# A hybrid decoder step on one core: prompt attention with a logits buffer per query tile, and its masks and divisions issued in rows

## The chip, the cores and the metric

The kernel runs on one core of a Trainium2 chip. The core has a matmul engine (TensorE, PE in the profile), a vector engine (VectorE, DVE), a scalar engine (ScalarE, ACT), GpSimd (POOL) and a sync engine (SyncE, SP) that here only starts transfers. The metric is the device time of one execution in microseconds, as the median over runs.

## The reference, cut to what matters

Two layers, each with four head groups side by side, an output projection and a mixture of experts. The change concerns group A, sparse attention, for a prompt of 512 tokens and for a sample group of 8 sequences with 4 new tokens and 512 cached keys each.

```python
def dsa_attend(q, qi, wi, k, v, ki, q_pos, topk):
    dots = jnp.einsum('bthd,bsd->bths', qi.astype(f32), ki.astype(f32)) * IDX_DIM ** -0.5
    score = jnp.einsum('bth,bths->bts', wi.astype(f32), jax.nn.relu(dots))
    ...
    _, sel = lax.top_k(score, topk)
    ...
    logits = jnp.einsum('bthd,btkhd->bthk', q.astype(f32), k_sel.astype(f32)) * A_HEAD_DIM ** -0.5
    logits = jnp.where(valid[:, :, None, :], logits, -jnp.inf)
    p = jax.nn.softmax(logits, axis=-1)
    return jnp.einsum('bthk,btkhd->bthd', p.astype(v.dtype), v_sel)
```

Group B (a recurrence called rwkv below) ends with a norm over its heads, `y = ((y - mu) * rsqrt(var + eps)) * g + b`, a bonus and a gate. Its last steps are interleaved with the attention in the code.

## The kernel before

Each engine runs a program of its own, written out by hand; order on an engine is program order, and engines meet at named semaphores. There is no scheduler. `m.*` are fixed places in one SBUF arena, `ps` is the PSUM with 8 banks.

The selected keys are a bias (0 or a large negative number) that is added to dense logits. The prompt has 4 query tiles of 128 tokens; tile i looks at i + 1 key tiles, for 4 heads. Its steps are:

- `logits(i)` on PE (L1051): 4 matmuls into `ps` banks 0 to 3.
- `masked(i)` on DVE (L2239 for tiles 0 and 1, L2243 for 2 and 3, then L2246): adds the bias into `m.lg`, then takes the row maximum into `m.nmax`.
- `exps(i)` on ACT (L1534): the exponentials in place, with the row sums.
- `normed(i)` on DVE (L2252, L2254): reciprocal of the sum, and the division in place.
- `output(i)` on PE: per head a transpose of the probabilities (L1070), and `values(i, h)` (L1059), the product with V. ACT's `turned(i)` (L1292, the helper of every copy) takes each transpose out of PSUM, and ACT's `output(i)` the result; with it PE's count `pv_mm` goes up by one per tile.

Tiles 0 and 2 share one `m.lg` buffer and one set of statistics, tiles 1 and 3 the other.

The sample group comes in two halves g of 4 sequences. Its cached keys are 16 pages a half; SP starts one transfer for each (L444, 128 KB, into `m.K[g]`), half 0 first, after the recurrence is done. `sample_logits` on PE (L1108 to L1115) does both halves in a row, and half g starts with

```python
pe.wait_ge((s["k0_in"], s["k1_in"])[g], nth(l, f"k{g}_in", 256))
```

that is, with all 16 pages of its half. ACT copies them to `m.s_lg[g]`, DVE takes the maximum (L2270, `s_max`), ACT the exponentials (L1562, `s_exp`), DVE divides (L2274, L2276, `s_p`), and `sample_attention` on PE (L1126 to L1142) transposes and multiplies with the cached values, which POOL starts to load (L599) when the recurrence is done.

Behind this stand the output projection (L1174 for the sample rows, L1185 for the prompt's) and, on SP, its weights, 4 MB into the region of the logits buffers:

```python
sp.wait_ge(s["pv_mm"], nth(l, "pv_mm", 4))
sp.dma_start(m.wout, layer_of(din["wout"], l)).then_inc(s["wout_in"], 16)
```

`y_centred`, `y_rates`, `y_scaled` and `y_out` on DVE are the last steps of the norm of group B (L2104 to L2124); `y_out` must be done before the output projection.

Of the kernel before, what the change touches and what calls it, by code (L numbers as in the profile page):

```python
# [16 lines left out]
ALU = mybir.AluOpType  # L17
ACT = mybir.ActivationFunctionType
AX = mybir.AxisListType
# [6 lines left out]
PAST, PAGE = 512, 128  # L26
# [162 lines left out]
def nth(l, name, n):  # L189

    return l * PER_LAYER[name] + (n + START.get(name, 0))
# [10 lines left out]
def memory(arena):  # L202
# [33 lines left out]
    m.ln = view(LN0, 2, DM)  # L236

    st = view(SM0, 680)
    m.nmax, m.ssum, m.rsum = ([st[:, 8 * k + 4 * j:8 * k + 4 * j + 4] for j in range(2)] for k in range(3))
    m.lam = [st[:, 24 + 2 * k:26 + 2 * k] for k in range(8)]  # L240
    m.minus_lam = st[:, 532:534]
    m.bn, m.mv, m.std = [view(SM0 + 44, 2, 6), view(SM0 + 666, 2, 6)], [st[:, 56:58], st[:, 58:60]], [st[:, 664:665], st[:, 665:666]]
# [78 lines left out]
    m.wb_in, m.sums, m.QI = view(TAIL, 4, P), view(TAIL + 512, 4, 32), view(TAIL + 640, 2, 4, DS)  # L321
    m.top8 = [view(SM0 + 500 + 8 * k, 8) for k in range(4)]
    assert TAIL + 672 <= R2 + 12288 and 7 * TP + CW <= 8 * DM
    m.lg, m.pT = [view(R1, 4, 384), view(R1 + 4096, 4, PAST)], [view(R1 + 6144, 4, 384), view(R1 + 1536, 4, PAST)]
    m.s_lg, m.s_pT = ([view(R4 + at + w * k, w) for k in range(2)] for at, w in ((0, T), (2 * T, PAST)))
    m.s_pTn, m.s_o = ([view(R4 + at + w * k, w) for k in range(2)] for at, w in ((2 * T + 2 * PAST, P), (2368, WA)))
    m.K = [view(at, 2, 4, PAST) for at in (R2, XT0)]
# [309 lines left out]
def tensor_program(pe, s, m, ps):  # L637
# [404 lines left out]
    def prompt_attention(l):  # L1042

        def logits(i):
            if i >= 2:
                pe.wait_ge(s["lg_taken"], nth(l, "lg_taken", i))
            for h in range(4):
                q = slice(64 * (h % 2), 64 * (h % 2) + 64)
                w = P * (i + 1)
                a = (2 * i + h % 2, w * (h // 2)) if i < 2 else (h, 0)  # L1050
                mm = pe.matmul(ps[:, a[0], a[1]:a[1] + w], m.qT[q, h // 2, P * i:P * i + P], m.kT[q, h // 2, 0:P * (i + 1)],  # L1051
                               start=True, stop=True)
            mm.then_inc(s["lg_mm"], 1)

        def values(i, h):
            pe.wait_ge(s["pt_copied"], nth(l, "pt_copied", 4 * i + h + 1))
            q = slice(64 * (h % 2), 64 * (h % 2) + 64)
            for c in range(i + 1):
                mm = pe.matmul(ps[q, 6 + i % 2, P * (h // 2):P * (h // 2) + P], m.A[:, c, 512 + 64 * h:576 + 64 * h],  # L1059
                               m.pT[i % 2][:, h, P * c:P * c + P], start=c == 0, stop=c == i)  # L1060
            return mm

        def output(i):
            pe.wait_ge(s["p_ready"], nth(l, "p_ready", i + 1))
            for h in range(4):
                k = 4 * i + h
                if k >= 2:
                    pe.wait_ge(s["pt_copied"], nth(l, "pt_copied", k - 1))
                for c in range(i + 1):
                    mm = pe.transpose(ps[:, 4 + h % 2, P * c:P * c + P], m.lg[i % 2][:, h, P * c:P * c + P], ident)  # L1070
                mm.then_inc(s["pt_mm"], 1)
                if h == 0 and i >= 2:
                    pe.wait_ge(s["ya_copied"], nth(l, "ya_copied", i - 1))
                if h:
                    values(i, h - 1)
            values(i, 3).then_inc(s["pv_mm"], 1)

        pe.wait_ge(s["rw_a"], nth(l, "rw_a", len(RW_ACT)))
        pe.wait_ge(s["rw_v"], nth(l, "rw_v", len(RW_DVE)))
        y_sums(l, m.yb).then_inc(s["yn_mm"], 1)  # L1080
        y_gates(l, (7, 3), slice(0, SEQ))
        logits(0)
        pe.wait_ge(s["gate_out"], nth(l, "gate_out", 1))
        logits(1)
        pe.wait_ge(s["yn_in"], nth(l, "yn_in", 1))
        y_sums(l, m.y2)
        y_gates(l, (6, 6), slice(SEQ, T))
        pe.wait_ge(s["yn_std"], nth(l, "yn_std", 1))
        output(0)
        logits(2)  # L1090
        output(1)
        logits(3)
        output(2)
        sample_logits(l)
        output(3)

    def sample_logits(l):
# [192 lines left out]
def scalar_program(act, s, m, ps, din, dout):  # L1290
    def copy(out, in_):
        return act.activation(out, in_, ACT.Copy)  # L1292
# [236 lines left out]
    def attention(l):  # L1529
        def exps(i):  # L1530
            act.wait_ge(s["lg_ready"], nth(l, "lg_ready", i + 1))
            for h in range(4):
                x = m.lg[i % 2][:, h, 0:P * (i + 1)]
                ins = act.activation(x, x, ACT.Exp, bias=m.nmax[i % 2][:, h:h + 1], accum_out=m.ssum[i % 2][:, h:h + 1])  # L1534
            ins.then_inc(s["p_exp"], 1)

        def turned(i):
            for h in range(4):
                act.wait_ge(s["pt_mm"], nth(l, "pt_mm", 4 * i + h + 1))
                copy(m.pT[i % 2][:, h, 0:P * (i + 1)], ps[:, 4 + h % 2, 0:P * (i + 1)]).then_inc(s["pt_copied"], 1)  # L1540

        def output(i):
            act.wait_ge(s["pv_mm"], nth(l, "pv_mm", i + 1))
            copy(m.yT[:, 0:2, P * i:P * i + P], ps[:, 6 + i % 2, 0:256].rearrange("p (q n) -> p q n", q=2))\
                .then_inc(s["ya_copied"], 1)

        y_norm(l)
        exps(0)
        for i in range(NT):
            if i + 1 < NT:  # L1550
                exps(i + 1)
            else:
                for g in range(2):
                    act.wait_ge(s["s_lg_mm"], nth(l, "s_lg_mm", g + 1))
                    copy(m.s_lg[g][:, 0:PAST], ps[:, 2 - 2 * g, :])
                    copy(m.s_lg[g][:, PAST:T], ps[:, 3 - 2 * g, 0:NS]).then_inc(s["s_lg"], 1)
            turned(i)
            output(i)

        for g in range(2):  # L1560
            act.wait_ge(s["s_max"], nth(l, "s_max", g + 1))
            act.activation(m.s_lg[g], m.s_lg[g], ACT.Exp, bias=m.nmax[g][:, 0:1], accum_out=m.ssum[g][:, 0:1])\  # L1562
                .then_inc(s["s_exp"], 1)
        for g in range(2):
            act.wait_ge(s["s_pt_mm"], nth(l, "s_pt_mm", g + 1))
            copy(m.s_pT[g], ps[:, 4, :])
            copy(m.s_pTn[g][0:NS, :], ps[0:NS, 5, 0:P]).then_inc(s["s_pt"], 1)
        for g in range(2):
            act.wait_ge(s["s_pv_mm"], nth(l, "s_pv_mm", g + 1))
            copy(m.s_o[g], ps[:, 6 + g, 0:WA]).then_inc(s["s_o"], 1)  # L1570
        act.wait_ge(s["s_ot_mm"], nth(l, "s_ot_mm", 2))
        for p in range(2):
            for h in range(2):
                q, head = slice(64 * h, 64 * h + 64), DS * (2 * p + h)
                turned_back = ps[q, 2:4, P * p:P * p + P].rearrange("p g (j n) -> p g j n", j=4)
                ins = copy(m.yT[q, p, SEQ:T].rearrange("p (g j t) -> p g j t", g=2, t=DS), turned_back[:, :, :, head:head + DS])
        ins.then_inc(s["attn_done"], 1)
# [108 lines left out]
def vector_program(dve, s, m, ps):  # L1686
# [543 lines left out]
    def attention(l):  # L2230
        def masked(i):
            w = P * (i + 1)
            x = m.lg[i % 2][:, :, 0:w]
            bias = m.bias[3 - i] if i else m.const("causal")
            dve.wait_ge(s["lg_mm"], nth(l, "lg_mm", i + 1))
            if i >= 2:
                dve.wait_ge(s["pt_mm"], nth(l, "pt_mm", 4 * (i - 1)))
            if i < 2:
                ins = tt(x.rearrange("p (a b) n -> p a b n", b=2),  # L2239
                         ps[:, 2 * i:2 * i + 2, 0:2 * w].rearrange("p b (a n) -> p a b n", n=w),  # L2240
                         bias.unsqueeze(1).unsqueeze(1).broadcast_to([P, 2, 2, w]), add)
            else:
                ins = tt(x, ps[:, 0:4, 0:w], bias.unsqueeze(1).broadcast_to([P, 4, w]), add)  # L2243
            ins.then_inc(s["lg_taken"], 1)
            dve.drain()
            dve.tensor_reduce(m.nmax[i % 2], x, AX.X, ALU.max, negate=True).then_inc(s["lg_ready"], 1)  # L2246

        def normed(i):
            w = P * (i + 1)
            x = m.lg[i % 2][:, :, 0:w]  # L2250
            dve.wait_ge(s["p_exp"], nth(l, "p_exp", i + 1))
            dve.reciprocal(m.rsum[i % 2], m.ssum[i % 2])  # L2252
            dve.drain()
            tt(x, x, m.rsum[i % 2].unsqueeze(2).broadcast_to([P, 4, w]), mul).then_inc(s["p_ready"], 1)  # L2254

        y_centred(l)
        masked(0)
        masked(1)
        normed(0)
        y_rates(l, 0)  # L2260
        normed(1)
        masked(2)
        y_rates(l, 1)
        normed(2)
        masked(3)
        y_scaled(l)
        normed(3)
        for g in range(2):
            dve.wait_ge(s["s_lg"], nth(l, "s_lg", g + 1))
            dve.tensor_reduce(m.nmax[g][:, 0:1], m.s_lg[g], AX.X, ALU.max, negate=True).then_inc(s["s_max"], 1)  # L2270
        y_out(l)
        for g in range(2):
            dve.wait_ge(s["s_exp"], nth(l, "s_exp", g + 1))
# [397 lines left out]
```

## Time and profile before

| | us |
|---|---|
| median of 3 runs | 1508.06 (1507.02 to 1508.68) |
| profiled execution, its own time | 1512.3 |
| span of its trace | 1510.7 |
| PE busy | 1237.6 (82%) |
| DVE busy | 658.6 (44%) |
| ACT busy | 347.7 (23%) |
| POOL busy | 160.0 (11%) |

Busy times overlap, so they don't add up to the span. The prompt attention takes two short stretches of the span, about 327 to 391 in the first layer and 1062 to 1126 in the second; the sample attention goes on to about 407 and 1144. A time in a row of the trace is counted from the start of the span.

### The profile page before, as it was taken

How to read it: one execution, taken by the hardware profiler on the slowest of the kernel's cores; microseconds unless marked ns; L12 is line 12 of the kernel's file. 1: busy time of each engine (PE TensorE's matmuls, PEld its weight loads, DVE VectorE, ACT ScalarE, POOL GpSimd, SP SyncE). 2: the span in 40 equal slices, each digit the busy share in tenths (PEclk: the TensorE clock that was granted, in tenths of full speed). 3: DMA queues.
4: the chain of work that ended last, by engine and by line, in shares of the span. 5: the costliest groups of instructions: out<-in, count | busy, mean ns of one | idle time of the engine just before them, and what ended most of it. 6: DMA issues, size and time to landing. Idle time of an engine off the chain costs nothing.

```text
span 1510.7 us, 22279 instructions
## 1 busy us (share of the span) xinstructions
PE 1237.6 (82%) x8296; PEld 778.2 (52%) x8296; DVE 658.6 (44%) x1371; ACT 347.7 (23%) x806; POOL 160.0 (11%) x224
## 2 busy tenths in 40 slices
PE   4989999975898099999299899998679944999950
PEld 2566778943445044444156577797344532444420
DVE  0036898866144301111353469987632450111118
ACT  1134232213222011111143432320332210111110
POOL 0040007013000200000201000430310002000011
PEclk9988999986798589999699699999787966999985
DMA  6095210026530369998712021100547005999953
GB/s 253 7 388 218 70 57 18 4 62 174 210 160 1 139 222 358 360 369 318 276 49 75 15 66 60 30 19 3 157 149 299 1 0 194 328 373 365 360 183 131
DMA packets 67917, 246.30 MB, mean 163 GB/s; under 512 B 8722, under 2 KB 29362, under 8 KB 58674
## 3 DMA queue, kind: packets, MB, share of 16 engines
q1 hardware_dynamic: 48736, 177.17, 32.6%
q0 software_dynamic: 14048, 50.00, 9.3%
q10 hardware_dynamic: 5042, 17.90, 2.9%
q8 instruction: 60, 0.98, 0.3%
q14 instruction: 31, 0.25, 0.1%
HBM read 194.39 MB, written 52.87 MB: 164 GB/s over the span
## 4 chain that ended last, share of the span: by engine, by line
PE 73%; DVE 10%; ACT 4%; DMA 4%; issue 3%; SPq 3%; DVEq 2%; POOL 1%; POOLq 0%; ACTq 0%
PE ps L1222 15%; PE ps L691 12%; PE ps L824 10%; PE ps L1240 8%; PE ps L1185 7%; PE ps L671 7%; PE ps L1213 2%; SPq L444 1%; PE ps L750 1%; PE ps L1059 1%; DMA arena<-in_wa 1%; POOL rows_in L610 1%; ACT arena L1292 1%; SPq L441 1%; DVE arena L1833 1%
## 5 line engine op out<-in xcount | busy, mean ns | idle before, releaser
L1292 ACT ACTIVATE arena<-ps 128x512 f32<-128x512 f32 (+14 forms) x358 | 155.3, 469 | 701.8 <-PE ps L691 155.5
L691 PE MATMUL ps<-arena 128*128 128x272 f32 x1088 | 261.1, 400 | 0.0
L1222 PE MATMUL ps<-arena 128*128 128x512 f32 x512 | 231.7, 605 | 4.8 <-ACT arena L1292 4.8
L691 PEld LDWEIGHTS ps<-arena 128*128 128x128 f32 x1088 | 208.9, 193 | 50.5 <-issue 5.5
L1222 PEld LDWEIGHTS ps<-arena 128*128 128x128 f32 x512 | 98.8, 194 | 131.2 <-issue 131.2
L824 PE MATMUL ps<-arena 64*64 64x64 f32 (+3 forms) x4016 | 151.3, 235 | 12.5 <-DVE arena L2050 10.3
L824 PEld LDWEIGHTS ps<-arena 64*64 64x64 f32 x4016 | 137.7, 137 | 25.2 <-issue 13.7
L671 PE MATMUL ps<-arena 128*128 128x512 f32 (+1 forms) x256 | 105.5, 572 | 22.5 <-DMA arena<-in_wa 19.4
L1240 PE MATMUL ps<-arena 128*128 128x512 f32 x256 | 117.7, 602 | 3.8 <-DVE arena L2499 3.8
L1185 PE MATMUL ps<-arena 128*128 128x512 f32 x256 | 112.4, 594 | 0.0
L2499 DVE COPY arena<-ps 128x256 f32<-128x256 f32 x32 | 13.6, 426 | 188.1 <-PE ps L1229 188.1
L671 PEld LDWEIGHTS ps<-arena 128*128 128x128 f32 x256 | 49.5, 196 | 74.6 <-issue 74.6
L1213 PE MATMUL ps<-arena 128*128 128x128 f32 x256 | 35.0, 282 | 58.0 <-DMA arena<-rows_in 58.0
L1185 PEld LDWEIGHTS ps<-arena 128*128 128x128 f32 x256 | 47.5, 189 | 56.6 <-issue 56.5
L2505 DVE COPY arena<-ps 128x512 f32<-128x512 f32 x32 | 22.2, 693 | 119.5 <-PE ps L1240 119.5
L1240 PEld LDWEIGHTS ps<-arena 128*128 128x128 f32 x256 | 45.8, 189 | 52.5 <-issue 48.0
L1213 PEld LDWEIGHTS ps<-arena 128*128 128x128 f32 x256 | 30.3, 145 | 59.3 <-DMA arena<-rows_in 58.2
L1590 ACT ACTIVATE arena<-ps,arena 128x128 f32<-128x128 f32 (+1 forms) x120 | 41.6, 453 | 65.7 <-PE ps L1154 45.7
L1619 ACT ACTIVATE arena<-ps 128x256 f32<-128x256 f32 x32 | 12.3, 386 | 188.0 <-PE ps L1222 188.0
L1059 PE MATMUL ps<-arena 128*64 128x128 f32 x160 | 30.0, 351 | 27.3 <-ACT arena L1292 27.3
L2193 DVE MATCH_REPLACE8 arena<-arena 32x544 f32<-32x544 f32 (+3 forms) x82 | 47.0, 586 | 0.0
L615 POOL TENSOR_TENSOR arena<-arena 128x1 f32<-128x1 f32 x2 | 0.4, 188 | 410.8 <-ACTq L1664 410.8
(343 smaller groups left out, 1323.9 us busy)
## 6 DMA issues: line engine op xcount, KB each, us to landing
arena<-in_w_gu SPq DMA_DIRECT2D x32, 2048.0 KB, 10.1
arena<-in_w_dn SPq DMA_DIRECT2D x32, 1024.0 KB, 9.5
arena<-in_wf SPq DMA_DIRECT2D x34, 512.0 KB, 3.7
arena<-rows_in SPq DMA_DIRECT2D x32, 512.0 KB, 9.6
rows_out<-arena ACTq DMA_DIRECT2D x32, 512.0 KB, 8.5
rows_in<-arena POOLq DMA_DIRECT2D x12, 1024.0 KB, 24.2
arena<-in_cache_v POOLq DMA_DIRECT2D x64, 128.0 KB, 2.7
arena<-in_cache_k SPq DMA_DIRECT2D x64, 128.0 KB, 2.8
```

The costliest lines, as they stand in the source:

```text
L671: mm = pe.matmul(ps[:, k % 2, 0:w], m.xT[:, c, row_tile(i)], m.wa[:, c, a:a + w], start=c == 0, stop=c == KC - 1)
L691: mm = pe.matmul(ps[:, 2 + 2 * h + n % 2, 0:HALF], m.wf[n % 3][:, c, :], m.xT[:, c, h * HALF:h * HALF + HALF], start=c == 0, stop=c == KC - 1)
L824: mm = pe.matmul(out[q], lhsT[q], rhs[q], start=start, stop=stop, skip_group_check=check)
L1059: mm = pe.matmul(ps[q, 6 + i % 2, P * (h // 2):P * (h // 2) + P], m.A[:, c, 512 + 64 * h:576 + 64 * h], m.pT[i % 2][:, h, P * c:P * c + P] ...
L1185: mm = pe.matmul(ps[:, 2 * (i % 2) + h, :], m.yT[:, c, row_tile(i)], m.wout[:, c, 512 * h:512 * h + 512], start=c == 0, stop=c == 7)
L1213: mm = pe.transpose(ps[:, c // 4, P * (c % 4):P * (c % 4) + P], m.xg[k][:, P * c:P * c + P], ident)
L1222: mm = pe.matmul(ps[:, 3 + k, :], m.xgT[:, c, :], m.w_gu[k][:, c, :], start=c == 0, stop=c == KC - 1)
L1240: mm = pe.matmul(ps[:, 5 + h, :], m.hT[:, f, :], m.w_dn[k][:, f, 512 * h:512 * h + 512], start=f == 0, stop=f == 1)
L1292: return act.activation(out, in_, ACT.Copy)
L1590: ins = act.activation(m.xT[:, c, P * i:P * i + n], ps[:, 4 + c // 4, n * (c % 4):n * (c % 4) + n], ACT.Identity, bias=m.lnc[:, 1, c:c + 1 ...
L2193: dve.match_replace(m.score[c][rows], m.top8[c][rows], m.score[c][rows], TAKEN)
L2505: dve.tensor_copy(m.y[k][:, 512:DM], ps[:, 6, :]).then_inc(s["y_copied_v"], 1)
```

## The change

`m.lg` becomes four buffers, one per query tile, and the statistics four sets; DVE's wait for the transposes of tile i - 2 before it writes tile i's logits is gone. DVE issues three masks in a row, then three divisions, then the mask and the division of tile 3; the two long reciprocals of group B's norm (L2111) stand before and after the last division, and `y_scaled` behind the maxima of the sample group. ACT issues the exponentials of three tiles in a row, and the sample group's steps stand between those of tiles 1, 2 and 3. PE issues `logits(2)` before `output(0)`, `logits(3)` before `output(1)`, and `sample_logits` before `output(2)`.

```diff
-    m.nmax, m.ssum, m.rsum = ([st[:, 8 * k + 4 * j:8 * k + 4 * j + 4] for j in range(2)] for k in range(3))
+    m.nmax, m.ssum, m.rsum = ([st[:, a + 8 * k + 4 * j:a + 8 * k + 4 * j + 4] for a in (0, 536) for j in range(2)]
+                              for k in range(3))
...
-    m.lg, m.pT = [view(R1, 4, 384), view(R1 + 4096, 4, PAST)], [view(R1 + 6144, 4, 384), view(R1 + 1536, 4, PAST)]
+    m.lg = [view(at, 4, P * (i + 1)) for i, at in enumerate((R1 + 7680, LN0, R1, R1 + 4096))]
+    m.pT = [view(R1 + 6144, 4, 384), view(R1 + 1536, 4, PAST)]
...
         y_gates(l, (6, 6), slice(SEQ, T))
+        logits(2)
         pe.wait_ge(s["yn_std"], nth(l, "yn_std", 1))
         output(0)
-        logits(2)
+        logits(3)
         output(1)
-        logits(3)
+        sample_logits(l)
         output(2)
-        sample_logits(l)
         output(3)
...
         y_norm(l)
-        exps(0)
-        for i in range(NT):
-            if i + 1 < NT:
-                exps(i + 1)
-            else:
-                for g in range(2):
-                    act.wait_ge(s["s_lg_mm"], nth(l, "s_lg_mm", g + 1))
-                    copy(m.s_lg[g][:, 0:PAST], ps[:, 2 - 2 * g, :])
-                    copy(m.s_lg[g][:, PAST:T], ps[:, 3 - 2 * g, 0:NS]).then_inc(s["s_lg"], 1)
-            turned(i)
-            output(i)
-
+        for i in range(3):
+            exps(i)
+        turned(0)
+        output(0)
+        turned(1)
+        output(1)
+        exps(3)
+        for g in range(2):
+            act.wait_ge(s["s_lg_mm"], nth(l, "s_lg_mm", g + 1))
+            copy(m.s_lg[g][:, 0:PAST], ps[:, 2 - 2 * g, :])
+            copy(m.s_lg[g][:, PAST:T], ps[:, 3 - 2 * g, 0:NS]).then_inc(s["s_lg"], 1)
+        turned(2)
+        output(2)
         for g in range(2):
             act.wait_ge(s["s_max"], nth(l, "s_max", g + 1))
             act.activation(m.s_lg[g], m.s_lg[g], ACT.Exp, bias=m.nmax[g][:, 0:1], accum_out=m.ssum[g][:, 0:1])\
                 .then_inc(s["s_exp"], 1)
+        turned(3)
+        output(3)
...
             dve.wait_ge(s["lg_mm"], nth(l, "lg_mm", i + 1))
-            if i >= 2:
-                dve.wait_ge(s["pt_mm"], nth(l, "pt_mm", 4 * (i - 1)))
...
         y_centred(l)
-        masked(0)
-        masked(1)
-        normed(0)
+        for i in range(3):
+            masked(i)
+        for i in range(3):
+            normed(i)
+        masked(3)
         y_rates(l, 0)
-        normed(1)
-        masked(2)
+        normed(3)
         y_rates(l, 1)
-        normed(2)
-        masked(3)
-        y_scaled(l)
-        normed(3)
         for g in range(2):
             dve.wait_ge(s["s_lg"], nth(l, "s_lg", g + 1))
             dve.tensor_reduce(m.nmax[g][:, 0:1], m.s_lg[g], AX.X, ALU.max, negate=True).then_inc(s["s_max"], 1)
+        y_scaled(l)
         y_out(l)
```

The rest of the diff replaces `m.lg[i % 2][:, h, 0:w]`, `m.nmax[i % 2]`, `m.ssum[i % 2]` and `m.rsum[i % 2]` by those of tile i.

Two places in the instruction order carry the argument. First PE around `sample_logits`, in the first layer. Line numbers of the changed kernel are 2 higher there: L1108 to L1115 of before are L1110 to L1117, a transpose L1070 is L1072, a product with V L1059 is L1061. Before:

```order
L1059 MATMUL ps<-arena 64x128 x6
L1108 MATMUL ps<-arena 32x512 x8
L1110 MATMUL ps<-arena 128x512
L1113 MATMUL ps<-arena 128x32 x2
L1115 MATMUL ps<-arena 128x32
L1108 MATMUL ps<-arena 32x512 x8
L1110 MATMUL ps<-arena 128x512
L1113 MATMUL ps<-arena 128x32 x2
L1115 MATMUL ps<-arena 128x32
L1070 MATMUL ps<-arena 128x128 x8
L1059 MATMUL ps<-arena 64x128 x4
```

The six L1059 at the top end `output(2)`; the eight L1070 at the bottom (4 key tiles for 2 heads) begin `output(3)`. The same place of the changed kernel:

```order
L1061 MATMUL ps<-arena 64x128 x4
L1110 MATMUL ps<-arena 32x512 x8
L1112 MATMUL ps<-arena 128x512
L1115 MATMUL ps<-arena 128x32 x2
L1117 MATMUL ps<-arena 128x32
L1110 MATMUL ps<-arena 32x512 x8
L1112 MATMUL ps<-arena 128x512
L1115 MATMUL ps<-arena 128x32 x2
L1117 MATMUL ps<-arena 128x32
L1072 MATMUL ps<-arena 128x128 x6
L1061 MATMUL ps<-arena 64x128 x3
```

The four L1061 at the top end `output(1)`, and the six L1072 at the bottom (3 key tiles for 2 heads) begin `output(2)`: both halves of `sample_logits`, with the waits for the cached keys, have moved ahead of one tile's whole output.

Second ACT around the sample group's exponentials (128x544, L1562 of before, L1565 of the changed kernel), with the semaphores that each instruction waits for. Before:

```order
L1292 ACTIVATE arena<-ps 128x384 [waits pt_mm] x4
L1292 ACTIVATE arena<-ps 128x2x128 [waits pv_mm]
L1292 ACTIVATE arena<-ps 128x512 [waits s_lg_mm]
L1292 ACTIVATE arena<-ps 128x32
L1292 ACTIVATE arena<-ps 128x512 [waits s_lg_mm]
L1292 ACTIVATE arena<-ps 128x32
L1292 ACTIVATE arena<-ps 128x512 [waits pt_mm] x4
L1292 ACTIVATE arena<-ps 128x2x128 [waits pv_mm]
L1562 ACTIVATE arena<-arena 128x544 [waits s_max] x2
L1292 ACTIVATE arena<-ps 128x512 [waits s_pt_mm]
```

The 128x384 copies are `turned(2)`, the four 128x512 that wait for `pt_mm` are `turned(3)`. The changed kernel:

```order
L1294 ACTIVATE arena<-ps 128x512 [waits s_lg_mm]
L1294 ACTIVATE arena<-ps 128x32
L1294 ACTIVATE arena<-ps 128x512 [waits s_lg_mm]
L1294 ACTIVATE arena<-ps 128x32
L1294 ACTIVATE arena<-ps 128x384 [waits pt_mm] x4
L1294 ACTIVATE arena<-ps 128x2x128 [waits pv_mm]
L1565 ACTIVATE arena<-arena 128x544 [waits s_max] x2
L1294 ACTIVATE arena<-ps 128x512 [waits pt_mm] x4
L1294 ACTIVATE arena<-ps 128x2x128 [waits pv_mm]
L1294 ACTIVATE arena<-ps 128x512 [waits s_pt_mm]
```

The copies of the sample logits now stand ahead of `turned(2)`, and the two exponentials ahead of `turned(3)` in place of behind it.

## Rows read from the trace of the kernel before

**Rows 1.** Page, chain that ended last, shares by engine and by line.

```profile
PE 73%; DVE 10%; ACT 4%; DMA 4%; issue 3%; SPq 3%; DVEq 2%; POOL 1%; POOLq 0%; ACTq 0%
```

**Rows 2.** Chain of waits, first layer: start, duration, engine and line.

```profile
380.34 1.87 PE ps L1108 x16
...
384.19 1.19 ACT arena L1292 x3
...
385.43 1.09 PE ps L1059 x8
...
388.72 1.80 PE ps L1059 x16
...
392.58 0.63 PE ps L1126 x4
...
407.01 6.08 PE ps L1174 x64
```

**Rows 3.** Chain of waits, second layer, the same columns.

```profile
1112.89 3.08 DMA arena<-in_cache_k
...
1116.02 1.95 PE ps L1108 x16
...
1119.95 1.20 ACT arena L1292 x3
...
1128.68 1.02 PE ps L1126 x4
...
1144.28 6.08 PE ps L1174 x64
```

**Rows 4.** Timeline, SP's starts of the 32 key pages in each layer.

```profile
329.68 47.34 SPq L444 DMA_DIRECT2D arena<-in_cache_k  x32
...
1065.42 48.03 SPq L444 DMA_DIRECT2D arena<-in_cache_k  x32
```

**Rows 5.** Last three key transfers of the first layer: issue, and time to landing.

```profile
L444 SPq DMA_DIRECT2D arena<-in_cache_k x3: 565/565/565, 373.6 to 376.5; - x3
...
DMA to landing us min/median/max: 2.3/2.4/2.4
```

**Rows 6.** Output projection's weights, both layers: issue, and time to landing.

```profile
L449 SPq DMA_DIRECT2D arena<-in_wout x2: 352/355/358, 390.5 to 1126.3; - x2
...
DMA to landing us min/median/max: 12.1/12.6/13.2
```

**Rows 7.** Chain of waits, first layer: third logits' start, output(2)'s first and last products.

```profile
360.68 2.01 PE ps L1051 x8
...
370.77 1.54 PE ps L1059 x6
...
375.06 1.46 PE ps L1059 x12
```

**Rows 8.** Windows of 1 us: length, PE busy, granted clock, DMA share, GB/s.

```profile
368.00:369.00 1.00, 0.00 (x0) 0.50 0.61 177
...
371.00:372.00 1.00, 1.00 (x6) 0.50 0.52 162
...
374.00:375.00 1.00, 1.00 (x7) 0.79 0.09 26
...
389.00:390.00 1.00, 1.00 (x12) 1.00 0.00 0
...
395.00:396.00 1.00, 1.00 (x14) 0.50 0.83 360
```

**Rows 9.** Windows, second layer's sample attention: PE, PEld, DVE, ACT, POOL, clock, DMA, GB/s.

```profile
1128.60:1136.00 7.40, 6.48 (x48) 3.03 (x49) 0.51 (x2) 0.75 (x2) 0.00 (x0) 0.51 0.99 426
1136.00:1142.00 6.00, 5.16 (x44) 1.77 (x42) 0.00 (x0) 1.01 (x3) 0.00 (x0) 0.50 0.65 266
```

**Rows 10.** Timeline, ACT between output(3)'s copy and the end of the sample exponentials.

```profile
390.54 0.39 ACT L1292 ACTIVATE arena<-ps 128x256 f32<-128x256 f32 x1 [1.18 <-PE ps L1059]
...
392.19 0.19 ACT L1562 ACTIVATION_READ_ACCUMULATOR arena<-arena 128x1 f32 x1
```

More of the change, by code:

```diff
@@ L1069, in output @@
                 for c in range(i + 1):
-                    mm = pe.transpose(ps[:, 4 + h % 2, P * c:P * c + P], m.lg[i % 2][:, h, P * c:P * c + P], ident)
+                    mm = pe.transpose(ps[:, 4 + h % 2, P * c:P * c + P], m.lg[i][:, h, P * c:P * c + P], ident)
                 mm.then_inc(s["pt_mm"], 1)
@@ L1532, in exps @@
             for h in range(4):
-                x = m.lg[i % 2][:, h, 0:P * (i + 1)]
-                ins = act.activation(x, x, ACT.Exp, bias=m.nmax[i % 2][:, h:h + 1], accum_out=m.ssum[i % 2][:, h:h + 1])
+                x = m.lg[i][:, h, :]
+                ins = act.activation(x, x, ACT.Exp, bias=m.nmax[i][:, h:h + 1], accum_out=m.ssum[i][:, h:h + 1])
             ins.then_inc(s["p_exp"], 1)
@@ L2232, in masked @@
             w = P * (i + 1)
[L2233 removed]
+            x = m.lg[i]
             bias = m.bias[3 - i] if i else m.const("causal")
             dve.wait_ge(s["lg_mm"], nth(l, "lg_mm", i + 1))
[L2236 to L2237 removed]
             if i < 2:
@@ L2245, in masked @@
             dve.drain()
-            dve.tensor_reduce(m.nmax[i % 2], x, AX.X, ALU.max, negate=True).then_inc(s["lg_ready"], 1)
+            dve.tensor_reduce(m.nmax[i], x, AX.X, ALU.max, negate=True).then_inc(s["lg_ready"], 1)
         def normed(i):
             w = P * (i + 1)
-            x = m.lg[i % 2][:, :, 0:w]
+            x = m.lg[i]
             dve.wait_ge(s["p_exp"], nth(l, "p_exp", i + 1))
-            dve.reciprocal(m.rsum[i % 2], m.ssum[i % 2])
+            dve.reciprocal(m.rsum[i], m.ssum[i])
             dve.drain()
-            tt(x, x, m.rsum[i % 2].unsqueeze(2).broadcast_to([P, 4, w]), mul).then_inc(s["p_ready"], 1)
+            tt(x, x, m.rsum[i].unsqueeze(2).broadcast_to([P, 4, w]), mul).then_inc(s["p_ready"], 1)
         y_centred(l)
-        masked(0)
-        masked(1)
-        normed(0)
+        for i in range(3):
[3 more added lines that the diff above has]
+        masked(3)
         y_rates(l, 0)
-        normed(1)
-        masked(2)
+        normed(3)
         y_rates(l, 1)
-        normed(2)
-        masked(3)
-        y_scaled(l)
-        normed(3)
         for g in range(2):
```

## The prediction

> **What bounds the kernel now.** I read the page's chain first: PE holds 73% of what ends last, DVE 10%, transfers 4% [rows 1]. So a change here counts where PE waits inside the two attention stretches, and I followed the chain of waits through them in order of time, then went to the timeline for what the chain waits on.
>
> In the second layer the chain does not run through the prompt's masks at all. It runs through the starts of the cached keys: the last page is started at 1112.89, has landed 3.08 us later, and at 1116.02 PE begins the second half of `sample_logits` [rows 3]. SP needs 48.03 us to start 32 pages, 1.50 each; in the first layer 47.34 us, 1.48 each [rows 4]. There the last page is started at about 376.5 and lands 2.4 later, at 378.9 [rows 5], while PE, which comes from `output(2)`, takes up that half at 380.34 [rows 2]. So before, two things meet within 1.4 us in the first layer and exactly in the second: PE done with tiles 0 to 2, and the keys there. From then on the order is: second half of `sample_logits`, `output(3)`, sample attention, output projection.
>
> The change doesn't touch what SP starts or when: these transfers wait for the recurrence alone. Whatever it wins ahead of them ends in a wait for `k1_in`. What counts is how much PE work then stands behind that wait, and this is what the change alters.
>
> **The change part by part.** Let S be the end of `sample_logits`: 384.2 before in the first layer, 1119.95 in the second [rows 2, 3].
>
> *Masks in a row, four buffers, DVE's dropped wait, `logits` one tile early, the long reciprocals moved.* All of it lies before S. Before, `output(1)` ended at 360.7, where the third logits begin [rows 7]; with any gain it ends there or earlier, and PE then does the first half of `sample_logits` (3.85 us, from 380.34 to 384.2 for its twin) and stands until 378.9. I cost these edits at nothing: 14 us of waiting hide them. If that cover were gone, it would be because the keys came sooner, which is the first rival.
>
> *`sample_logits` ahead of `output(2)`.* PE is in order, so `output(2)` and `output(3)` stand behind the wait for `k1_in`. Before, only `output(3)` did.
>
> 1. Start of the second half: 378.9 in place of 380.3 in the first layer, -1.4; the same 1116.0 in the second, 0.
> 2. Clock. A PE that has stood that long comes back at half of its clock: it shows 0.50 at 368, when it had no work, and keeps it at 371, when work was back; only at 374, where the mean is 0.79, does it rise [rows 8]. `output(2)`'s products started at 370.77 [rows 7], so about 3.65 us ran at 1.2 GHz and not at 2.4. The same here costs 1.8 us. Bounds: 0, if the clock came back at once, and 3.85, if the whole half ran at half clock. I take 1.8, the only row that restarts on work of this kind.
> 3. `output(2)` after S. The copies by ACT come first, as they do before for `output(3)`: S to the first products is 1.2 us (384.2 to 385.4) [rows 2]. Its products and transposes take 370.77 to 376.52, 5.75 us, of which 3.65 at half clock [rows 7, 8]; at full clock that is 1.8 + 2.1 = 3.9. End: S + 5.1.
> 4. `output(3)`. Now ACT has the result's copy and the two sample exponentials ahead of `turned(3)`: 390.54 to 392.38, 1.84 us [rows 10], and a copy of 128x512 (0.6) before the first products: 2.5 in all. Then 385.43 to 390.52, 5.1 us [rows 2]. End: S + 12.7; before it was S + 6.35.
> 5. Sample attention starts at once, since its exponentials are done by then: S + 12.7 in place of S + 8.4 (392.58) and S + 8.7 (1128.68) [rows 2, 3]: +4.3 and +4.0. The exponentials' move thus gives back some 2 us of the 6.35 that `output(2)` puts on the path.
>
> Start of the sample attention: -1.4 + 1.8 + 4.3 = +4.7 in the first layer, 0 + 1.8 + 4.0 = +5.8 in the second.
>
> *A credit, from the clock.* Before, PE stood from 390.5 to 392.6, and the clock fell in the course of the sample attention: 0.50 at 395 [rows 8], 0.51 from 1128.6 [rows 9]. That pause goes. In the second layer PE was busy 6.48 us and then 5.16 us at half clock in it [rows 9], so full clock would give back between 0 and 5.8. I take the first of the two rows, 3.2, because a pause for ACT's copies stays in each half and may bring the clock down again. In the first layer the stretch took 14.4 and not 15.6 us [rows 2, 3], so 1.2 of that is had already: credit 2.0. This makes +2.7 and +2.6.
>
> *The weights of the output projection.* SP starts them at the end of `output(3)`. That moves by -1.4 + 1.8 + 6.35 = +6.8 in the first layer and by 8.2 in the second. They land 12.1 to 13.2 us after their start [rows 6]; with the shorter in the first layer and the longer in the second that is 402.6 + 6.8 = 409.4 and 1139.5 + 8.2 = 1147.7, against 407.01 and 1144.28 where the projection began [rows 2, 3]: at least +2.4 and +3.4. This floor is what a faster sample attention runs into. It decides in the second layer.
>
> *`y_scaled` and `y_out`* move behind the maxima of the sample group and end some 7 us after S; the sample divisions behind them on DVE aren't wanted before S + 12.7, the projection far later. Nothing, with 5 us of cover. The norm weights behind the projection's on SP are used only in the norm after it.
>
> **Sum**: 2.7 + 3.4 = +6.1 us. The profiled execution, 1512.3 us with a span of 1510.7, would become 1518.4; it was itself 4.2 above the median, so I carry the difference over: 1508.06 + 6.1 = 1514.2.
>
> **The rivals.**
>
> *Faster: the keys don't hold PE.* If they landed early enough, `sample_logits` would start at 360.7 at the latest, end 7.7 later at 368.4, and the sample attention would start at 381.1 in place of 392.6: -11.5 a layer, -23 in all, 1485. For it: POOL's and SP's loads share the transfer engines at about 0.6 of their time [rows 8], so there is bandwidth. Against it: the pace is that of SP's own starts [rows 4], which no edit reaches. It decides from a landing about 5 us earlier than now (373.9 and 1110). Chance 0.05.
>
> *The clock gives nothing back.* Sample attention at half clock again: 4.7 + 5.8 = +10.5, 1518.6; with the whole second half of `sample_logits` at half clock 2.0 more a layer, 1522.6. For it: the pauses for ACT within the sample attention remain, and those before ran at 0.50 though PE was busy 6.48 of 7.40 us [rows 9]. Chance 0.2.
>
> *The clock gives back all.* Full clock to the end of the projection's sample rows, whose 6.08 us [rows 2, 3] would become about 3: the floor of 5.8 less 6, 1508. Against it: waiting for the weights is a pause of its own. Chance 0.12, half of it within 0.2%.
>
> *Transposes don't keep the clock up.* If they counted for nothing, `output(2)` and `output(3)` would run at half clock: 3.9 + 5.1 more a layer, +18, 1532. Against it: the clock rose in the middle of transposes and products [rows 7, 8] and stood at 1.00 at 389, in the middle of `output(3)` [rows 8]. Chance 0.03. This is what the Trainium skill, "TensorE: Matmul & The Clock Gate", section "Part 4: PE-mode transpose", would have: a transpose doesn't count as PE-busy in the same way, and full clock doesn't engage for it. The rows speak against it, for a mix of one transpose to two products at least.
>
> *The change doesn't reach the end.* A few us late here could be taken up by a transfer that is waited for later (4% of the chain [rows 1]): 1508. I see none between here and the experts. Chance 0.08.
>
> **How the numbers follow.** Forecast 0.52 (+4 to +8), nothing back 0.2 (+8 to +14.5), all back 0.12 (0 to +4), keys early 0.05, transposes 0.03, absorbed 0.08. The likeliest is 1514.2, its own range 1512 to 1516. Out to 1510 and 1520 (+2 to +12) the range takes in most of the two clock cases, the unknown there, and leaves about 2 in 10 out. Within 0.2% (3 us, about what a measurement of this kernel can tell from no change): absorbed and half of "all back", 0.14; faster 0.05; slower the rest, 0.81.
>
> **What would show it.** In the changed kernel's trace: PE idle from some 361 to 379 and from about 1098 to 1116, and the wait there put down to the cached keys in both layers; the clock at 0.50 when it comes back; the first products of `output(2)` behind that; ACT's sample exponentials between the copies of tiles 2 and 3; no pause of 2 us ahead of the sample attention; the projection's weights started at about 397 and 1134.5, and PE waiting for them or nearly so. The forecast is wrong if the keys land more than 1 us sooner or later against the end of the recurrence, if PE's idle stretch is missing, or if `output(2)` and `output(3)` take more than 13 us after S.

## The result, and the profile after

| | before | after |
|---|---|---|
| median of 4 runs each | 1508.37 (1507.02 to 1509.71) | 1521.25 (1519.88 to 1523.54) |
| profiled execution, its own time | 1512.3 | 1520.68 |
| span of its trace | 1510.7 | 1519.0 |
| PE busy | 1237.6 | 1224.5 |

The changed kernel takes 1.0083 times as long, 95% interval 1.007 to 1.0096: 12.9 us slower. The forecast was +6.1, with a range up to 1520. The sign and the place are right, the size forecast is less than half of it, and the time lies outside the range. Against the profiled execution of before the difference is 8.4, against the median 12.9. The 4.5 between the two count below.

A second execution of the kernel before was traced (1507.56 us, span 1505.9), and one of the changed kernel (1522.05, span 1520.4). The four traces by stage, each stage ended by the first matmul of the next: to the end of the recurrence; the attention stretch, up to the output projection's first sample row; on to the second recurrence's end; the second stretch; the rest.

| us | to recurrence | stretch 1 | between | stretch 2 | rest |
|---|---|---|---|---|---|
| before, as in the rows above | 326.9 | 80.1 | 655.4 | 81.9 | 366.4 |
| before, traced again | 326.4 | 81.0 | 654.7 | 78.1 | 365.7 |
| after | 325.9 | 83.0 | 656.1 | 87.9 | 366.1 |
| after, traced again | 327.1 | 82.9 | 656.3 | 88.0 | 366.1 |

The loss is in the two stretches. With the second trace of before as base it is 2.0 and 9.8, with the first 2.9 and 6.0.

A stretch ends where the projection's first sample row begins, and the 64 matmuls of these rows don't always take the same time: 6.57 and 3.66 us in the two layers of before's second trace, 5.35 and 5.60 in that of after. Counted to the end of these rows, after is 0.8 us longer in the first layer and 11.7 in the second. These 12.5 us account for nearly all of the 12.9. The experiments below are counted in the same way, each against before's second trace ("to the rows' end").

The page of after, the chain by engine, answers to [rows 1]:

```profile
PE 69%; DVE 9%; DMA 6%; SPq 5%; issue 4%; ACT 3%; DVEq 2%; POOL 1%; POOLq 0%; ACTq 0%
```

Transfers went from 4% to 6%, SP's own starts from 3% to 5%: PE ends less of the chain, and it waits more. The waits of PE, after, summed over the span (us in total, times, longest):

```profile
PE ps L1215 <- DMA arena<-rows_in: 58.1, 2, 29.2
PE ps L1110 <- DMA arena<-in_cache_k: 39.4, 2, 20.6
```

The first wait is the experts' and was there before at 58.0. The second is `sample_logits`: 39.4 us in two waits, one a layer. In before's second trace PE waits for these keys once, for 0.3 us. Where the two waits of after lie, from the timeline of PE, after (start, duration, what, and in brackets the idle time before it and who ended it):

```profile
355.24 1.94 PE L1110 MATMUL ps<-arena 128*32 128x512 f32 x16
...
377.94 3.66 PE L1110 MATMUL ps<-arena 128*32 128x512 f32 x16 [18.80 <-DMA arena<-in_cache_k]
...
1117.99 3.67 PE L1110 MATMUL ps<-arena 128*32 128x512 f32 x16 [20.60 <-DMA arena<-in_cache_k]
```

`output(1)` ends at 355.2 where it ended at 360.7 before [rows 7]; counted from the recurrence's end, 29.3 us and 33.8. So the edits ahead of the wait do win 4.5 us there. PE then does the first half of `sample_logits` at full speed (1.94 for its main matmuls) and stands 18.8 us. The second half takes 3.66 for the same work: half clock. What follows, in the chain of waits of after, first layer (start, duration, engine and line):

```profile
375.45 2.44 DMA arena<-in_cache_k
...
377.94 3.66 PE ps L1110 x16
...
383.83 1.08 ACT arena L1294 x3
...
389.07 0.39 ACT arena L1294
389.46 1.46 ACT arena L1565 x4
...
391.45 1.09 PE ps L1061 x8
...
396.56 12.31 DMA arena<-in_wout
...
408.90 5.35 PE ps L1176 x64
```

This answers to [rows 2]. Everything from 383.83 on is `output(2)` and `output(3)` behind the keys; the sample exponentials (L1565) stand between them; then the chain goes to the weights of the projection, started at 396.56 and not at 390.5 [rows 6], and no longer through the sample attention. The second layer, which answers to [rows 3]:

```profile
1115.52 2.43 DMA arena<-in_cache_k
...
1117.99 3.67 PE ps L1110 x16
...
1125.21 1.47 PE ps L1072 x6
...
1132.07 0.39 ACT arena L1294
...
1139.55 13.30 DMA arena<-in_wout
...
1152.90 5.60 PE ps L1176 x64
```

From the keys to the weights' start it is 18.6 us in the first layer (377.94 to 396.56) and 21.6 in the second (1117.99 to 1139.55), for the same instructions. The six transposes that begin `output(2)` (L1072) take 1.47 here and end later than ACT's copies; in the first layer the chain runs through those copies (383.83). Two windows of the sample attention, after (length, PE, PEld, DVE, ACT, POOL busy, granted clock, DMA share, GB/s), against [rows 9]:

```profile
396.60:408.90 12.30, 7.13 (x94) 3.40 (x93) 0.00 (x0) 3.26 (x11) 0.00 (x0) 1.00 0.92 374
1139.60:1152.90 13.30, 7.13 (x95) 3.40 (x94) 0.00 (x0) 3.26 (x11) 0.00 (x0) 0.89 0.93 378
```

PE needs 7.13 us for it, where [rows 9] show 6.48 + 5.16 = 11.64 at 0.50. It then waits 3.4 and 4.4 us for the weights. In the second layer the clock falls in that pause and is at 0.50 to 0.51 from 1152.9 to 1156.9; in the first it falls behind the pause (0.68 as the mean over the sample rows). These rows (L1176) take 5.35 and 5.60 us, where runs below show 3.66 at 1.00.

### The profile page after: what moved, and what is told of

Read it like the earlier page. It is cut to its first block, busy times and chain, and to the rows that moved or that the text cites. A ratio compares the mean times of both kernels' runs of the same rounds, so it can differ in the third digit from the quotient of the medians.

```text
span 1519.0 us, 22275 instructions
## 1 busy us (share of the span) xinstructions
PE 1224.5 (81%) x8296; PEld 771.6 (51%) x8296; DVE 659.4 (43%) x1371; ACT 348.5 (23%) x806; POOL 160.3 (11%) x224
## 4 chain that ended last, share of the span: by engine, by line
PE 69%; DVE 9%; DMA 6%; SPq 5%; issue 4%; ACT 3%; DVEq 2%; POOL 1%; POOLq 0%; ACTq 0%
PE ps L1224 15%; PE ps L693 12%; PE ps L826 10%; PE ps L1242 7%; PE ps L1187 7%; PE ps L673 7%; SPq L446 3%; SPq L443 2%; PE ps L1215 2%; DMA arena<-in_wout 2%; PE ps L752 1%; DMA arena<-in_wa 1%; POOL rows_in L612 1%; PE ps L1061 1%; DVE arena L1838 1%
## 5 line engine op out<-in xcount | busy, mean ns | idle before, releaser
L826 PE MATMUL ps<-arena 64*64 64x64 f32 (+3 forms) x4016 | 151.4, 235 | 12.5 <-DVE arena L2055 10.3
L2191 DVE MAX8 arena<-arena 32x8 f32<-32x544 f32 (+3 forms) x82 | 43.2, 589 | 1.2 <-issue 0.3
```

The costliest lines, as they stand in the source:

```text
L826: mm = pe.matmul(out[q], lhsT[q], rhs[q], start=start, stop=stop, skip_group_check=check)
L2191: dve.max(m.top8[c][rows], m.score[c][rows])
```

## The experiments

Times are medians; ratios are to runs of the kernel before that were taken beside them on the same chip. Their medians were 1507.38 (17 runs), 1507.83 (11) and 1508.14 (11). The last of these is from another chip than the other two and belongs to the run with 20 products and to the changed kernel's second trace. Lines of a kernel shift by a few where it has lines of its own: the main matmul of `sample_logits` is L1108, L1110, L1112 or L1114.

**One line moved in the kernel before.** Theory: the loss comes from PE's `sample_logits` ahead of `output(2)`, and from nothing else in the diff. Rival: the masks in a row, or the order on ACT and DVE, cost part of it.

```diff
         logits(3)
-        output(2)
         sample_logits(l)
+        output(2)
         output(3)
```

> The kernel before with one edit alone: PE does sample_logits ahead of output(2). Buffers, masks, divisions and ACT's order are those of before. Keys theory (output(2) and output(3) both stand behind the wait for the cached keys, and the weights of the output projection behind them): slower than before by 8 to 12 us, PE idle some 15 us ahead of the second half of sample_logits in each layer. Rival (the masks and divisions in a row, or the exponentials ahead of turned(3), delay the rest): within 2 us of before.

Measured: 1517.61 (1513.60 to 1519.28), ratio 1.0062 [1.0042, 1.0082]: 10.2 us slower. The stretches are 83.7 and 88.3 in its trace, as in the changed kernel (83.0 and 87.9). PE's timeline at the wait, and the second layer's chain:

```profile
1114.96 3.67 PE L1108 MATMUL ps<-arena 128*32 128x512 f32 x16 [10.98 <-DMA arena<-in_cache_k]
```

```profile
1136.16 13.34 DMA arena<-in_wout
...
1150.17 3.66 PE ps L1174 x64
```

The wait for the keys is 11.0 us here (10.4 in the first layer, where 15 were expected) and 20.6 in the changed kernel, where the masks are done sooner. PE's restart at half clock is the same (3.67). So the one moved line makes the stretches as long as the whole change does, and what the rest of the diff wins ahead of the keys ends in the wait.

It isn't the whole loss. To the rows' end this trace is 10.0 us longer than before's, close to the 10.2 of the medians, and the changed kernel's 12.5. The sample rows make the difference: they take 3.66 here in both layers. ACT's exponentials are where they were, the sample attention is done later, and PE stands 0.9 us ahead of the projection with the clock at 1.00. In the changed kernel it stands 3.4 and 4.4 us for the weights, and the clock falls. (Its trace is 6.1 us longer than this one in all; the other 3.6 or so lie in stages that neither edit touches, and what makes them isn't known.)

**The changed kernel with `sample_logits` back behind `output(2)`.** ACT's sample copies go back behind `output(2)`, its exponentials behind `output(3)`; four buffers, masks and divisions in rows, and the reciprocals stay as changed.

```diff
         output(1)
-        sample_logits(l)
         output(2)
+        sample_logits(l)
         output(3)
```

> The changed kernel with sample_logits back behind output(2) on PE, and ACT's sample copies behind output(2), its sample exponentials behind output(3), as before. Four buffers, masks and divisions in a row stay. Keys theory: output(2) fits into the wait for the keys; the half clock after the wait still costs 2 to 3 us a layer where PE now stands longer, so 1507 to 1514, 7 us or more below the changed kernel. Rival (masks and divisions in a row): stays at 1517 or above.

Measured: 1510.24 (1505.99 to 1513.36, 12 runs), ratio 1.0015 [1.0003, 1.0028]. Stretches 81.5 and 81.7 in the trace. Of 12.9 us 2 to 3 remain, and whether these are real is at the edge of the interval; to the rows' end it is 1.1 in the trace, which is of the shortest run. So the rest of the diff wins next to nothing, as costed: it makes PE earlier ahead of a wait. Second layer of the chain:

```profile
1113.33 3.67 PE ps L1110 x16
...
1120.55 1.90 PE ps L1072 x8
...
1128.65 13.28 DMA arena<-in_wout
...
1142.09 3.66 PE ps L1176 x64
```

With `output(2)` done, PE still waits for the keys, and comes back at half clock here too (3.67, and 1.90 for eight transposes): the price of the restart, without 5 to 7 us of `output(2)` behind it.

**Exponentials behind `output(3)`.** The changed kernel with ACT's two sample exponentials where they were. Theory: their move gave back some 2 us by starting the sample attention sooner. Rival: the weights end last, and the exponentials stand in the way of `turned(3)`.

```diff
         output(2)
+        turned(3)
+        output(3)
         for g in range(2):
             act.wait_ge(s["s_max"], nth(l, "s_max", g + 1))
...
                 .then_inc(s["s_exp"], 1)
-        turned(3)
-        output(3)
```

> The changed kernel with the two sample exponentials back behind turned(3) and output(3) on ACT. If the weights of the output projection end last in both layers (they land 3.4 and 4.4 us after PE is done with the sample attention in the changed kernel's trace), then output(3) ends 1.2 us sooner in each layer, the weights too, and the sample attention's later start (2 us) is hidden: faster than the changed kernel by about 2.5 us. If the sample attention ends last: slower by about 1 to 2 us a layer.

Measured: 1516.72 (1515.21 to 1517.68), ratio 1.0056 [1.0039, 1.0074]; 9.3 slower than before, against 12.9 of the changed kernel, which was not run beside it. The stretches are 83.2 and 87.0, so -0.7 in all. First the first layer, then the second:

```profile
395.71 0.39 ACT arena L1294
...
409.37 3.66 PE ps L1176 x64
```

```profile
1138.78 13.47 DMA arena<-in_wout
...
1152.29 3.66 PE ps L1176 x64
```

In the first layer the exponentials hold the sample attention, which ends last again: the stretch wins nothing. In the second the weights start 73.5 us after the recurrence and not 74.5, and end last. So in the stretches the exponentials' move costs up to 1 us where the weights end last, and gives back nothing.

Behind the stretches it costs more. Here PE stands 0.9 us ahead of the projection in the first layer and 2.4 in the second, the clock stays at 1.00, and the sample rows take 3.66 in both, against 5.35 and 5.60 in the changed kernel. To the rows' end this kernel is 8.1 us longer than before and the changed one 12.5. The whole trace is only 3.0 shorter than the changed kernel's, because the stage behind the first layer's rows is 1.5 longer here for a cause that isn't known. So the move was expected to give back some 2 us a layer and costs about 3 in all (3.0 by the traces, 3.6 by the medians, whose intervals overlap).

**PE kept busy in the wait.** Theory: a part of the loss is the half clock after the wait. 36 products of 128x128 by 128x512 into a bank that is free, ahead of the wait for the second half's keys; nothing reads them.

```diff
         for g in range(2):
+            for _ in range(36 if g else 0):
+                pe.matmul(ps[:, 4, :], ident, m.kT[:, 0, 0:SEQ], start=True, stop=True)
             pe.wait_ge((s["k0_in"], s["k1_in"])[g], nth(l, f"k{g}_in", 256))
```

> The changed kernel with 36 matmuls of 128x128 by 128x512 on PE ahead of the wait for the second half's keys; their result, in a PSUM bank that is free there, is used by nobody. About 15.4 us at full clock, in an idle stretch of 18.8 and 20.6 us. Clock theory (the half clock after the wait lengthens the second half of sample_logits by 1.9 and 3.3 us, and in the second layer output(2) by 1.5): PE comes back at full clock, output(3) and with it the weights of the output projection end 2 us earlier in the first layer and 4.5 in the second, faster than the changed kernel by 5 to 7 us. If the clock is not what lengthens them: same time as the changed kernel.

Measured: 1537.33 (1535.98 to 1539.21), ratio 1.0195 [1.0177, 1.0213]. It says nothing on the clock's price, since the filling was too long. PE's timeline:

```profile
359.55 31.19 PE L1105 MATMUL ps<-arena 128*128 128x512 f32 x72
390.68 1.94 PE L1112 MATMUL ps<-arena 128*32 128x512 f32 x16
```

Each product is two records in the trace, 0.87 us together, so 36 took 31.19 us and ended some 12 us behind the keys. What it does show: at full clock the second half's main matmuls take 1.94.

**The same with 20 of them**, which end ahead of the keys.

> As the kernel with 36 such matmuls, but 20: there each took 0.87 us (31.19 us for 36 at full clock), so that they ran 11 to 12 us past the landing of the keys. 20 take 17.3 us and end 1 to 3 us before the keys in both layers. Clock theory: second half of sample_logits in 3.9 us in place of 5.8 and 7.2, output(2) in the second layer 1.5 sooner, the weights of the projection started 2 and 4.8 us earlier than in the changed kernel: 5 to 7 us faster than it, 1514 to 1516. If the clock is not what lengthens them: the same as the changed kernel.

Measured: 1518.06 (1511.91 to 1519.23), ratio 1.0061 [1.004, 1.0082]: 9.9 slower than before, 3.2 less than the changed kernel's median, where 5 to 7 were expected. The traced run took 1513.51. In its trace the stretches are 82.2 and 81.8: -0.8 and -6.1. Second layer:

```profile
1117.78 1.95 PE ps L1112 x16
...
1134.44 12.35 DMA arena<-in_wout
...
1146.83 5.15 PE ps L1178 x64
```

Keys to weights' start is 16.7 us here and 21.6 in the changed kernel, so in this trace the half clock's share of the second stretch is 4.9 us; the weights took 12.35 and not 13.30, about 1 more. In the first layer 16.7 (379.56 to 396.23) against 18.6: 1.9, of which the stretch shows 0.8, because the weights took 13.39 there. The six runs fall into two groups, 1511.9 to 1513.5 (two, with the traced one, mean clock 0.904) and 1517.8 to 1519.2 (four, 0.901). What the longer ones lose isn't known: only a short one was traced, so the 4.9 us are shown for that execution and not for the median.

**Keys in fewer starts.** Theory: the keys' landing holds PE, and its pace is that of SP's starts. The second half's keys come in 8 transfers of 256 KB and not in 16 of 128 KB, from pages at fixed places and not by the page table, so the output for these four sequences is computed from other keys.

```diff
-        for g in range(2):
+        for g in range(1):
             with sp.Fori(0, 4) as j:
...
+        sp.wait_ge(s["state_out"], nth(l, "state_out", 64))
+        for j in range(4):
+            for q in range(2):
+                sp.dma_start(m.K[1][:, q, j, :].rearrange("p (z k) -> p z k", z=NPAGE),
+                             din["cache_k"][l * NPHYS + 4 * j:l * NPHYS + 4 * j + 4, :, q, :].rearrange("z p k -> p z k"))\
+                    .then_inc(s["k1_in"], 16)
```

> The changed kernel, but the second half's cached keys come in 8 transfers of 256 KB of fixed pages in place of 16 of 128 KB by the page table (so part of the output is of other keys). SP is done with its starts some 12 to 17 us earlier. Keys theory: PE waits little or not between the halves of sample_logits, the attention ends 10 to 14 us earlier a layer than in the changed kernel: 1492 to 1500, below the kernel before. If the keys don't hold PE: the same as the changed kernel, 1521.

Measured: 1493.54 (1487.99 to 1498.21), ratio 0.9906 [0.9883, 0.9929]: 14.3 us faster than before, 28 faster than the changed kernel. Stretches 70.2 and 73.9. First layer:

```profile
358.81 8.11 DMA arena<-in_cache_k
...
366.96 3.23 PE ps L1114 x16
...
384.91 12.14 DMA arena<-in_wout
```

Counted from the recurrence's end, the keys land 12.0 us sooner (366.92 here, 377.89 in the changed kernel), and the weights start 12.7 sooner: all of it passes on. PE still waits 6.7 us (6.9 in the second layer), for the transfers themselves now (8.11 from start to landing). To the rows' end this kernel is 14.2 us shorter than before. So whether the change's order is good or bad hangs on the time at which these keys land. Before's order was not run with early keys; its second trace leaves it little to win by them, since PE waits 0.3 us for the keys there.

**The halves apart.** If the work behind the wait is the price, then only the second half should stand behind it. From the changed kernel: the first half's logits ahead of `output(2)`; then `output(2)`, `output(3)`, the first half's attention; the second half's logits, softmax and attention last. ACT and DVE follow the same order; nothing is left out.

```diff
         output(1)
-        sample_logits(l)
+        sample_logits(l, 0)
         output(2)
         output(3)
...
         for g in range(2):
+            if g:
+                sample_logits(l, 1)
             pe.wait_ge(s["pt_copied"], nth(l, "pt_copied", 16))
```

> The changed kernel with the halves of the sample group taken apart on PE, ACT and DVE: the first half's logits ahead of output(2), then output(2), output(3), the first half's whole attention, and only then the wait for the second half's keys, with its logits, softmax and attention behind it. Nothing is left out. Keys theory: output(2), output(3) and the first half fit into the wait, the weights of the projection start before the keys land; behind the wait stand 4 to 6 us of logits, about 4 of softmax and 6 of attention, so the projection starts some 14 to 17 us after the keys land, in place of 31 to 35 in the changed kernel: 16 us earlier a layer, 1485 to 1495, faster than both kernels. If the keys are not what holds PE: no faster than before.

Measured: 1487.43 (1484.09 to 1488.98), ratio 0.9857 [0.9835, 0.9878]: 20.4 us faster than before, 34 faster than the changed kernel. Stretches 68.7 and 70.5; to the rows' end 12.9 and 7.6 shorter than before, 20.5 in all. The first layer's chain, then the projection's weights (issue, and who waited):

```profile
376.54 3.11 DMA arena<-in_cache_k
...
379.69 1.95 PE ps L1110 x16
...
386.82 1.08 PE ps L1130 x4
...
395.74 5.98 PE ps L1178 x64
```

```profile
L451 SPq DMA_DIRECT2D arena<-in_wout x2: 426/430/433, 377.3 to 1104.0; - x2
...
who waited for it (us, times):
busy tenths in 40 slices 0000000000000000000000000000000000000000
```

The keys land as late as ever (379.65), but PE stood 0.46 us for them and not 18.8 (3.10 and not 20.6 in the second layer). The weights start at 377.3, ahead of the keys' landing, and nobody waits for them. Behind the keys stand one half's logits, softmax and attention, 16 us.

## Why the prediction was wrong in size

**Right: the mechanism, its place, the sign.** PE stands from 359.1 to 377.9 and from 1097.4 to 1118.0 (forecast: some 361 to 379, 1098 to 1116). The edits ahead of the wait count next to nothing, which moving `sample_logits` back showed, and the one moved line carries 10.2 of the 12.9 us. Steps 3 and 4 hold in the first layer: from the end of `sample_logits` to the end of `output(3)` the forecast was 12.7 us, and it took 12.7 (383.83 to 396.56). In the second it took 14.3 (1125.21 to 1139.55), over the 13 that the prediction named as a sign of being wrong; the clock makes the difference (Wrong 2). The weights start at 396.56 in the first layer (forecast 397), and they end last in both, where the sum had them last in the second alone. The credit's cause came as written too: no pause ahead of the sample attention, and full clock in it.

**Wrong 1: the base.** "It was itself 4.2 above the median, so I carry the difference over" is the largest error: 8.4 against the profiled execution are 12.9 against the median. The profiled execution of before ran its second sample attention at half clock [rows 9], and the difference could not be carried over. The floor set 4.8 us against the later weights in the second layer, from their landing at 1139.5 to the projection at 1144.28. In the second trace of before, of a run near the median, only 0.8 of these are there. Second layer:

```profile
1115.88 1.95 PE ps L1108 x16
...
1126.16 13.27 DMA arena<-in_wout
1139.43 0.78 issue
1140.21 3.66 PE ps L1174 x64
```

The sample attention ran at a clock of 0.88 (8.91 us busy of 14.00, from 1126.2 to 1140.2), and the weights ended last in before already. The sample rows took 3.66 and not 6.08 [rows 3], the stretch 78.1 and not 81.9. Of 39 later runs of before six had the profiled execution's mean clock of 0.885; these took 1509.8 to 1512.7, and the median run is not among them. That all six had this half clock in the sample attention is likely but not shown, since they were not traced. In the execution near the median the second layer's projection begins 0.8 us behind the weights' landing, so nearly all that delays their start is lost.

**Wrong 2: the clock at the restart (step 2).** It was set at 1.8 us a layer. In the first layer the second half took 5.9 us (377.94 to 383.83) where full clock takes 3.85: 2.0, close to the 1.8. In the second layer the clock stayed down. Windows of 1 us of after, first the first layer, then the second:

```profile
380.00:381.00 1.00, 1.00 (x8) 0.00 (x0) 0.00 (x0) 0.00 (x0) 0.00 (x0) 0.50 0.00 0
...
382.00:383.00 1.00, 1.00 (x4) 0.20 (x3) 0.00 (x0) 0.00 (x0) 0.00 (x0) 0.97 0.00 0
```

```profile
1118.00:1119.00 1.00, 1.00 (x8) 0.37 (x12) 0.00 (x0) 0.00 (x0) 0.00 (x0) 0.50 0.00 0
...
1124.00:1125.00 1.00, 1.00 (x6) 0.94 (x5) 0.00 (x0) 0.00 (x0) 0.00 (x0) 0.50 0.00 0
...
1129.00:1130.00 1.00, 1.00 (x7) 0.86 (x6) 0.92 (x2) 0.49 (x1) 0.00 (x0) 0.71 0.00 0
1130.00:1131.00 1.00, 1.00 (x8) 0.80 (x8) 0.93 (x2) 0.38 (x1) 0.00 (x0) 1.00 0.00 0
```

The second half took 7.2 us (1117.99 to 1125.21), 3.4 over full clock, and `output(2)` 6.9 (to 1132.07) where the first layer took 5.2 (383.83 to 389.07), 1.6 over: 5.0 in place of 1.8. That is above the upper bound given for the step (3.85), since the bound stopped at the half's end and the low clock didn't. Filling the wait took 4.9 off this stretch between keys and weights in the execution that was traced, which is the same figure from the other side.

**Wrong 3: the pause ahead of the projection.** The prediction names it ("waiting for the weights is a pause of its own") but puts nothing for it into the sum, which ends where the projection begins. PE waited 3.4 and 4.4 us there, and the sample rows behind it took 5.35 and 5.60 us, against 6.57 and 3.66 in before's second trace: -1.2 and +1.9. Step 5's "The exponentials' move thus gives back some 2 us" failed by it: with the weights last, an earlier sample attention only lengthens this pause.

**The sum as it came out**, by the floor, which ended both layers, against before's second trace: the weights start 70.7 us after the recurrence and not 63.9 in the first layer, +6.8 (forecast 6.8), and 74.5 and not 64.0 in the second, +10.5 (forecast 8.2). The stretches add 2.0 and 9.8. In the second layer only 0.8 stood against the 10.5, PE's pause behind the weights' landing (1139.43). In the first the weights lay ready some 5 us ahead of the projection before (started at 390.2, 12.0 us under way, wanted at 407.4), and that took up 5.1 of the 6.8; the weights were 0.3 us longer under way after. With the sample rows (-1.2 and +1.9) it is 0.8 and 11.7. The forecast had 2.7 and 3.4. The first came near its 2.0 by luck: it was worked out for the sample attention ending last, and the weights did.

**The rivals.** "The keys don't hold PE" falls as a description of the change, and its price is borne out in part: keys landing 12 us sooner gave 14.3 against before, where -23 was worked out for keys that don't hold PE at all. "The clock gives nothing back" has the measured size (1518.6 to 1522.6), but not the mechanism: the sample attention did run at full clock. It came near the time because there was nothing to give back to the median run, and because the restart cost more. "The clock gives back all" had full clock to the end of the sample rows; these ran at half clock for the most part, after the pause that was named against it. "Transposes don't keep the clock up" falls: `output(2)` and `output(3)` took 12.7 us in the first layer, as worked out at full clock.

**Open.** Why the clock rose after 4 us of matmuls in the first layer and after 11.6 in the second. Both traces of after have it in the second layer (1119.4 to 1131.0 in the other one), so it is no accident of one execution; the same instructions run ahead of the rise, and the idle time ahead of them, 18.8 and 20.6 us, is nearly the same. It doesn't go with the layer either: with `sample_logits` back behind `output(2)` the first layer's clock stayed at 0.50 from 378.6 to 391, some 12 us, after an idle stretch of 10.2; and with the keys in fewer starts the second layer's rose 3.5 us after the restart (1093.1) and fell again at 1100.

## What to carry to other kernels

Before moving a wait ahead of work on an engine that runs in order, count what then stands behind that wait: what is won ahead of it is lost in it, and all that follows the work put behind it, with the starts of transfers that this work releases, is late by that work's length. An edit that lets the engine arrive sooner at its next wait can cost time too: here the work behind a longer pause ran at a lower clock. Where two inputs arrive at different times, take the work on them apart, so that only what needs the late one stands behind it; here that turned 12.9 us lost into 20.4 won. A forecast against a profiled execution that isn't a median one needs the stages in which it differs from the others before any of their slack is counted as a gain.

## What the runs showed of the hardware

After an idle stretch of 18.8 to 20.6 us the granted clock was 0.50 in both layers, and with PE busy in each window from the restart on it came back after 4 us in the one and 11.6 in the other, in both traces of the changed kernel. After a pause of 2.7 us ahead of the same work, with the wait filled, the clock was still full (1.95 us for the second half's main matmuls in the second layer). The Trainium skill, "TensorE: Matmul & The Clock Gate", section "Part 4: PE-mode transpose", has full clock not engage for transposes. The rows bear it out no more than in the prediction: the clock was at 0.50 through 7.2 us of the second layer without one transpose, and it rose in the midst of `output(2)`'s transposes and products. What held it down in the second layer stays open. A product of 128x128 by 128x512 in f32 stands in the trace as two records and took 0.87 us, which is why the first filling of the wait was too long.
